# Column norms, split state-space output and set-up, a w_pg begun by quarters, and a later RWKV bonus in a two-block fp32 transformer kernel

## The reference

```python
h = h + rms_norm_2(mix, post_mix_norm[i])
u = rms_norm_2(h, pre_ffn_norm[i])
up = causal_dwconv(u @ w_up[i], conv_w[i], conv_b[i])
f = (gelu(gate) * val) @ w_down[i]
h = h + rms_norm_2(f, post_ffn_norm[i])
e = p[i] @ w_ple[i]
h = h + rms_norm_2(sigmoid(h @ w_ple_gate[i]) * e, ple_norm[i])
```

## Time and profile before

| | us |
|---|---|
| median of the runs | 3297.18 |
| the profiled execution | 3302.57 |
| its span | 3300.5 |
| TensorE busy | 3008.8 (91%) |
| VectorE busy | 2265.7 (69%) |
| ScalarE busy | 1621.3 (49%) |
| GpSimd busy | 324.4 (10%) |

### The profile page before, as it was taken

How to read it: one execution, slowest core, us unless ns; L and a number is a source line. 1 busy time by engine, 2 the same in 40 slices (tenths; PEclk the granted TensorE clock), 3 DMA queues, 4 the chain that set the end, 5 groups by cost and what they waited for, 6 DMA issues and landing times.

```text
span 3300.5 us, 60057 instructions
## 1 busy us (share of the span) xinstructions
PE 3008.8 (91%) x24264; PEld 2777.6 (84%) x24264; DVE 2265.7 (69%) x3538; ACT 1621.3 (49%) x2407; POOL 324.4 (10%) x569
## 2 busy tenths in 40 slices
PE   6799898879998988999898999989899999999987
PEld 2577777768888888999787889989899999999987
DVE  6367776587688876775565566666688855887565
ACT  3345555345466653745343432544555544555554
POOL 0012222100122221300000000010000000000000
PEclk8799999989999998999899998999899999999989
DMA  9876656755644445555232232535355555554543
GB/s 379 287 243 225 203 209 223 253 198 208 162 155 137 139 147 167 176 179 183 89 112 92 100 108 90 173 130 198 128 171 190 179 192 180 179 187 170 180 147 122
DMA packets 110708, 576.94 MB, mean 175 GB/s; under 512 B 33056, under 2 KB 33088, under 8 KB 46688
## 3 DMA queue, kind: packets, MB, share of 16 engines
q1 hardware_dynamic: 89040, 525.37, 45.2%
q0 software_dynamic: 20816, 44.27, 4.7%
q10 hardware_dynamic: 576, 3.47, 0.3%
HBM read 546.83 MB, written 17.83 MB: 171 GB/s over the span
## 4 chain that ended last, share of the span: by engine, by line
PE 60%; DVE 24%; ACT 6%; DMA 5%; issue 3%; SPq 1%; POOL 1%; DVEq 0%; ACTq 0%; POOLq 0%
PE acc L911 59%; DVE arena L871 7%; DVE rounded L871 6%; DVE arena L881 3%; ACT arena L908 2%; DVE upper L871 2%; DMA arena<-in_w_ada 2%; ACT rounded L908 2%; DMA arena<-in_w_in 1%; DVE upper L881 1%; ACT upper L908 1%; PE acc L914 1%; SPq L867 1%; DVE rounded L881 1%; DVE arena L877 1%
## 5 line engine op out<-in xcount | busy, mean ns | idle before, releaser
L911 PE MATMUL acc<-rounded 128*128 128x256 f32 x14688 | 1937.1, 291 | 52.6 <-issue 30.4
L911 PEld LDWEIGHTS acc<-rounded 128*128 128x128 f32 x14688 | 1843.6, 196 | 136.1 <-issue 100.3
L871 DVE TENSOR_TENSOR rounded<-arena,rounded 128x1024 fp32r<-128x1024 f32 (+1 forms) x832 | 1005.3, 1208 | 338.8 <-ACT rounded L908 271.0
L908 ACT ACTIVATE rounded<-arena 128x1024 fp32r<-128x1024 f32 (+1 forms) x864 | 883.6, 1023 | 648.7 <-PE acc L911 489.1
L911 PEld LDWEIGHTS acc<-upper_rounded,rounded 128*128 128x128 f32 x4560 | 565.3, 197 | 45.0 <-DVE rounded L871 22.8
L911 PE MATMUL acc<-upper_rounded,rounded 128*128 128x256 f32 x4560 | 573.1, 289 | 23.1 <-DVE rounded L871 20.7
L908 ACT ACTIVATE arena<-arena 128x256 f32<-128x256 f32 (+4 forms) x477 | 253.0, 530 | 306.0 <-DVE arena L871 213.9
L911 PE MATMUL acc<-arena 128*32 128x512 f32 (+8 forms) x1878 | 267.1, 467 | 79.9 <-DMA arena<-in_w_ada 42.7
L871 DVE TENSOR_TENSOR arena<-arena 128x256 f32<-128x256 f32 (+6 forms) x519 | 273.2, 526 | 51.7 <-ACT arena L908 30.1
L911 PEld LDWEIGHTS acc<-arena 128*32 128x32 f32 (+4 forms) x1878 | 122.8, 139 | 143.9 <-DMA arena<-in_w_ada 67.2
L871 DVE TENSOR_TENSOR arena<-acc,arena 128x256 f32<-128x256 f32 (+3 forms) x280 | 119.1, 425 | 178.0 <-PE acc L911 160.3
(11 more groups left out here) (90 smaller groups left out, 1165.3 us busy)
## 6 DMA issues: line engine op xcount, KB each, us to landing
arena<-in_w_in SPq DMA_DIRECT2D x164, 1024.0 KB, 5.0
arena<-in_w_ada SPq DMA_DIRECT2D x88, 1024.0 KB, 5.3
arena<-in_w_up SPq DMA_DIRECT2D x88, 1024.0 KB, 4.8
arena<-in_w_down SPq DMA_DIRECT2D x44, 1024.0 KB, 4.7
arena<-in_w_outa SPq DMA_DIRECT2D x16, 1024.0 KB, 7.3
arena<-in_w_glu SPq DMA_DIRECT2D x16, 1024.0 KB, 5.4
arena<-in_w_outm SPq DMA_DIRECT2D x16, 1024.0 KB, 5.0
arena<-in_w_out SPq DMA_DIRECT2D x16, 1024.0 KB, 4.8
```

Source lines behind the costliest of these rows:

```text
L871: return self.put(self.e and self.e.tensor_tensor(o, a, b, op))
L908: return self.put(self.e and self.e.activation(o, a, f, scale=scale, **kw))
L911: return self.put(self.e and self.e.matmul(o, l, r, start=start, stop=stop, skip_group_check=True))
```

## The change

- **Columns.** `rms` now multiplies the two halves of RS2 (as the stationary operand) by one column of ones: sums of the 256 tokens come as 128x2. Root and reciprocal work on 128x2 (NCOL). In `recip`, TensorE lays the two columns over all partitions into PSUM bank 3, and scaling reads them there. This holds for the tags (x, 0), mo, fo and em.
- **Early table.** `warm`, a Sqrt of one column, stands behind the first block of tile 15 of w_outm (both layers), w_out2 and w_down1.
- **Interleaving.** `post` is split into `scale` and `post`; the order is scale 0, post 0, scale 1, halves 0, post 1, scale 2, halves 1, and so on, where it was two of both ahead of the first halves.
- **Squares.** The three additions of squares for the w_up norm go from GpSimd to VectorE, as a background program in w_up's first 32 blocks.
- **Quarters.** w_pg's first 64 blocks take four tiles by four blocks of the contraction in turn; its weights are packed so.
- **S5.** Six more steps before block 0; the output is written, read back and passed through gelu in two halves, the first in a generator of its own as soon as block 7 is done; each `s5_out` is split in two parts, 8 steps a tile. Set-up is in 19 parts (two steps each in layer 1, where it was 8 parts; in layer 0 still 8 steps).
- **Bonus.** The bonus product, its multiplication by v and its spill go from stage 2 to stage 3; the subtraction for the exponentials goes from stage 3 to 2.

```diff
-PAIRS = (("w_in", 48), ("w_in2", 0), ("w_up", 0), ("w_pg", 0))
+PAIRS = (("w_in", 48), ("w_in2", 0), ("w_up", 0))
+QUADS = (("w_pg", 0),)
...
+            quads = (name, u0) in QUADS
+            if quads and blk < 64:
+                n, k = n0 + blk // 4 % 4, 4 * (blk // 16) + blk % 4
...
+            if (name, n, k) in (("w_outm", 15, 0), ("w_out2", 15, 0), ("w_down1", 15, 0)):
+                self.add("warm")
...
     def s5(self, l):
-        for i in range(8):
-            self.add("s5_setup", l, i)
-            yield
-            if l:
-                yield
+        for i, parts in enumerate((1, 2, 1, 4, 3, 2, 1, 5)):
+            for part in range(parts):
+                self.add("s5_setup", l, i, part)
+                if l or part == parts - 1:
+                    yield
+                if l:
+                    yield
...
         while ("u8", l, 0) not in self.marks:
             yield
+        for _ in range(6):
+            yield
...
-        self.add("s5_y", l)
-        for _ in range(20):
-            yield
-        for j in range(9):
-            self.add("s5_out", l, j)
...
+    def s5_back(self, l):
+        for half in range(2):
+            while ("s5", l, 8 * half + 7) not in self.marks:
+                yield
+            self.add("s5_y", l, half)
+            for _ in range(14):
+                yield
+            self.add("s5_yr", l, half)
+            for _ in range(8):
+                yield
+            for j in range(4 * half, 4 * half + 4):
+                self.add("s5_out", l, j, 0)
+                for _ in range(3):
+                    yield
+                self.add("s5_out", l, j, 1)
+                for _ in range(2):
+                    yield
+                self.add("part", ("ys", l), j)
+                for _ in range(3):
+                    yield
...
+    def scaled(self, tag, g):
+        if g == 0:
+            self.add("scale", tag, 0)
+        self.add("post", tag, g)
+        if g < 3:
+            self.add("scale", tag, g + 1)
+
+    def square_sums(self):
+        yield
+        for g in range(1, 4):
+            self.add("sum4", g)
+            yield
...
-        for g in range(5):
-            if g < 4:
-                self.add("post", "fo", g)
-            if g:
-                self.add("xs", g - 1)
+        for g in range(4):
+            self.scaled("fo", g)
+            self.add("xs", g)
...
-        pe.mm(B(3, 0, 256), con("ones"), V(RS2, 256), True, True).then_inc("norm_pe", tag)
+        for th in range(2):
+            x = pe.mm(B(3, th, 1), V(RS2 + 128 * th, 128), con("ones", 1), True, True)
+        x.then_inc("norm_pe", tag)
+
+    def recip(tag):
+        if tag in ("x0", "hf"):
+            return
+        pe.wait_ge("norm_dve", ("col", tag))
+        for th in range(2):
+            x = pe.mm(B(3, 128 * th, 128), V(NCOL + th, (0, 128)), con("ident"), True, True)
+        x.then_inc("norm_pe", ("over", tag))
...
-        if s == 2:
+        if s == 3:
             pe.wait_ge("rw_act", ("ld", i))
             pe.wait_ge("rw_dve", ("rk", i))
-            pe.mm(B(4, 0, 256), con("blk"), V(RT2, 256), True, True).then_inc("rw_pe", ("rk", i))
+            pe.mm(B(4, 0, 256), con("blk"), V(D2, 256), True, True).then_inc("rw_pe", ("rk", i))
...
+    def scale(tag, g):
+        src, stream, sem = {"mo": (MO, "w_out2", "ev_act"), "fo": (FO, "w_down1", "g_act"), "em": (EM, "w_pg", "g_act")}[tag]
+        t = V(src + 1024 * g, 4, 256)
+        dve.wait_ge(sem, ("ev", tl.out_of[stream, 0, 4 * g + 3].o))
+        dve.wait_ge("norm_pe", ("over", tag))
+        dve.tt(t, t, B(3, 0, (0, 4), (1, 256)), MUL)
```

More of the change, by code:

```diff
@@ L461, in stream @@
                 held.append(t)
-            if late is not None and blk == 39:
+            if late is not None and blk == (71 if quads else 39):
                 late()
@@ L715, in run @@
             self.stream("w_outa", l, 8 * l, 0, 16, 8, per=2)
-            self.drain(g5)
+            self.drain(g5, gy)
             self.add("glu_first", l)
@@ L1420, in rms, with warm @@
         act.wait_ge("norm_pe", tag)
-        act.act(V(RS, 256), B(3, 0, 256), ACT.Sqrt, bias=con("eps"), scale=1.0 / 2048).then_inc("norm_act", ("sqrt", tag))
+        if total is None:
+            to, sums = V(RS, 256), B(3, 0, 256)
+        else:
+            to, sums = V(NCOL, 2), B(3, 0, 2)
+        act.act(to, sums, ACT.Sqrt, bias=con("eps"), scale=1.0 / 2048).then_inc("norm_act", ("sqrt", tag))
+    def warm():
+        act.act(V(NCOL + 2, 1), con("eps"), ACT.Sqrt)
     def rms2():
@@ L1482, in part, with s5_setup @@
         act.act(to[0], V(src, 256), ACT.Copy).then_inc("part_act", key)
-    def s5_setup(l, i):
+    def s5_setup(l, i, part):
+        if part:
+            return
         if i == 0:
@@ L1857, in h @@
         for j in ([k] if k % 4 == 0 and l == 0 or k == 0 else []) + ([k + 1] if k < last else []):
-            dve.stt(V(UT + 256 * j, 256), V(X + 256 * j, 256), V(GP + j, 1), V(RS, 256), MUL, MUL).then_inc("h_dve", (l, j))
+            if l:
+                dve.wait_ge("norm_pe", ("over", ("x", 0)))
+            root = B(3, 0, 256) if l else V(RS, 256)
+            dve.stt(V(UT + 256 * j, 256), V(X + 256 * j, 256), V(GP + j, 1), root, MUL, MUL).then_inc("h_dve", (l, j))
         dve.wait_ge("h_act", (l, k))
@@ L1878, in part, with s5_setup @@
         low(to, V(src, 256), key)
-    def s5_setup(l, i):
-        if i == 1:
+    def s5_setup(l, i, part):
+        if i == 1 and part == 0:
             dve.wait_ge("s5_act", ("step", l))
@@ L1885, in s5_setup @@
             reduce_angle(V(IM, 64), V(TH, 64), V(T1, 64), 0.0)
+        if i == 1 and part == 1:
             dve.tt(V(TM, 64, 9), V(IM, (1, 64), (0, 9)), V(CON + CCOL["kk9"], (0, 64), (1, 9)), MUL)
             dve.tt(V(PK, 64, 9), V(RE, (1, 64), (0, 9)), V(CON + CCOL["kk9"], (0, 64), (1, 9)), MUL).then_inc("s5_dve", ("arg", l))
-        if i == 3:
+        if i == 3 and part == 0:
             dve.wait_ge("s5_act", ("pk", l))
@@ L1894, in s5_setup @@
             dve.stt(V(EM1, 64), V(EM1, 64), 2.0, V(T1, 64), MUL, MUL)
-            sin_arg(V(P1, 576), V(TM, 576), V(CC1, 576), con("ph1"), con("ph1r")).then_inc("s5_dve", ("p", l, 0))
-        if i == 4:
-            sin_arg(V(P2, 576), V(TM, 576), V(CC1, 576), con("ph2"), con("ph2r")).then_inc("s5_dve", ("p", l, 1))
-        if i == 5:
+        if i == 3 and part == 1:
+            turns_of(V(CC1, 576), V(TM, 576), con("ph1"))
+        if i == 3 and part == 2:
+            turned(V(P1, 576), V(TM, 576), V(CC1, 576))
+        if i == 3 and part == 3:
+            bounded(V(P1, 576), con("ph1r")).then_inc("s5_dve", ("p", l, 0))
+        if i == 4 and part == 0:
+            turns_of(V(CC1, 576), V(TM, 576), con("ph2"))
+        if i == 4 and part == 1:
+            turned(V(P2, 576), V(TM, 576), V(CC1, 576))
+        if i == 4 and part == 2:
+            bounded(V(P2, 576), con("ph2r")).then_inc("s5_dve", ("p", l, 1))
+        if i == 5 and part == 0:
             sin_arg(V(CO, 64), V(IM, 64), V(T1, 64), 0.25, con("hpi")).then_inc("s5_dve", ("trig", l, 0))
+        if i == 5 and part == 1:
             sin_arg(V(SI, 64), V(IM, 64), V(T1, 64), 0.0, con("zero")).then_inc("s5_dve", ("trig", l, 1))
@@ L1905, in s5_setup @@
             dve.tt(V(P2, 576), V(P2, 576), V(PK, 576), MUL)
-        if i == 7:
+        if i == 7 and part == 0:
             dve.wait_ge("s5_act", ("trig", l, 2))
@@ L1915, in s5_setup @@
             dve.recip(V(T1, 64), V(T1, 64))
+        if i == 7 and part == 1:
             dve.tt(V(QR, 64), V(CO, 64), V(ARE, 64), MUL)
@@ L1923, in s5_setup @@
             dve.tt(V(QI, 64), V(QI, 64), V(T1, 64), MUL)
+        if i == 7 and part in (2, 3):
             p1, p2 = V(P1, (9, 64), (1, 8)), V(P2, (9, 64), (1, 8))
             qr, qi = V(QR, (1, 64), (0, 8)), V(QI, (1, 64), (0, 8))
-            for j, (one, two, op) in enumerate(((p1, p2, ADD), (p2, p1, SUB))):
-                dve.tt(V(PQ + 512 * j, 64, 8), one, qr, MUL)
-                dve.tt(V(TM, 64, 8), two, qi, MUL)
-                dve.tt(V(PQ + 512 * j, 512), V(PQ + 512 * j, 512), V(TM, 512), op)
+            one, two, op = ((p1, p2, ADD), (p2, p1, SUB))[part - 2]
+            at = PQ + 512 * (part - 2)
+            dve.tt(V(at, 64, 8), one, qr, MUL)
+            dve.tt(V(TM, 64, 8), two, qi, MUL)
+            dve.tt(V(at, 512), V(at, 512), V(TM, 512), op)
+        if i == 7 and part == 4:
             dve.memset(V(KS, 960, np_=16), 0.0)
@@ L2604, in arrange @@
     order = np.concatenate([n, np.stack([16 + n, 24 + n, 32 + n, 40 + n], 1).reshape(-1), 8 + n])
-    A["w_in"] = np.concatenate([pack(w.reshape(2048, 48, 128)[:, order].reshape(2048, 6144)) for w in g["w_in"]])
+    A["w_in"] = np.concatenate([pack(w.reshape(2048, 48, 128)[:, order].reshape(2048, 6144))
+                                for w in g["w_in"]])
     A["w_outm"] = np.concatenate([pack(w[:1024]) for w in g["w_out"]])
```

160 lines of the change are left out of this document (82 added, 78 removed).

## The result

The changed kernel takes 3261.11 us (median of 4 runs, 3257.28 to 3263.28) against 3296.15 for the kernel before beside it: ratio 0.9889 (95% interval 0.9872 to 0.9906), 1.1% faster. The forecast was 3228, the range 3203 to 3262: the time lies 0.9 us inside the range's upper end, and the gain is half of the forecast one (35 of 69). The profiled execution took 3257.28, its span is 3255.5 against 3300.5: 45.0 us, where 70.5 were forecast.

The account below looks back on a forecast made before the run. TensorE's stream of weight products was bound by holes, most caused by VectorE, plus low clock after them. Terms 15 + 18 + 10 - 6.5 + 11 + 0 + 7.5 + 4.5 + 1 + 10 = 70.5 us off 3297.2; forecast 3228, range 3203 to 3262.

Parts of the forecast that it names:

- rival (a): VectorE is the true bound from 300 to 810 and 885 to 1303 us: 3252 us, chance 0.20.
- what was to show it wrong: Attention stretches longer by over 10 us each, or new waits for w_in in layer 0's first 100 products.
- What the first half costs: First-half gelu puts 12.5 us of VectorE into each attention stretch; 5 us lost in layer 1, 1.5 in layer 0.
- Six more steps: Before the first state-space block: 24 products ahead remove both waits for scr_u; 15 us gained (8 to 19).
- rival (c): State-space chain, shifted against the attention heads, meets their waits in another phase; up to 3315 us, chance 0.03.
- Output in halves: State-space output in w_outa: waits for scr_y and VectorE go; 18 us gained in layer 1, 10 in layer 0.
- Set-up: State-space set-up spread over 19 parts, 678.5 to 810.4 us: VectorE no longer solid; 11 us gained (3 to 19).
- Norm of layer 1's input: Root and reciprocal as columns, against table loads colliding with early sines: 0 (1.6 gained to 3 lost).
- Norms before w_up and w_pg: Earlier scaling and quicker first low halves: 7.5 us gained before w_up (3 to 9), 4.5 before w_pg (2 to 7).
- Tail: Last norm: reciprocal 1.75 becomes 0.18 us, a lay-over is added; 1.0 us gained (0.3 to 1.5).
- Later bonus: RWKV: bonus product one step later shortens TensorE's wait by 1.44 us, exponentials start sooner; 10 us gained (4 to 14).
- (b): Rival: with TensorE's holes the low clock goes too, fifteen us more gained; 3212 us, chance 0.13.

Follow-up runs that it names:

- e5: The kernel before with only the six more steps ahead of the first state-space block: 3297.27 us, ratio 1.0009.
- e6: The changed kernel with the first half's gelu tiles held until the attention's last head is done: 3240.54 us, ratio 0.9827.
- e8: The changed kernel with the first VectorE multiplication of each first-half gelu tile done five times: 3268.62 us, ratio 0.9907.
- e1: The changed kernel without the six steps ahead of the first state-space block: 3260.33 us, ratio 0.9887.
- e7: e6 with the six steps in layer 0 only: 3246.04 us, ratio 0.9841.
- e9: The changed kernel with layer 1's state-space set-up again in 8 parts and 16 steps: 3267.71 us, ratio 0.9904.
- e10: The kernel before with RWKV's subtraction for the exponentials ahead of VectorE's wait for the bonus product, which stays in stage 2: 3285.19 us, ratio 0.9967.

## Why the prediction was right or wrong

The time fell inside the range, but only just, and the mechanism failed in one step. Taken all at their ends, the bounds of the terms give 3192 to 3291, not 3205 to 3250, and the upper end of 3262 came from leaning toward rival (a). Of what was to show it wrong, attention stretches over 10 us longer each, came: 12.5 and 27.5. The other rows gained 85 for the 77 forecast, which hid 8 of the loss.

**What the first half costs** is the step that failed. It said that 12.5 us of VectorE enter each attention stretch and that 5 and 1.5 of them are lost. On their 96 products the four tiles of layer 1 cost 16.0 (e5 and e6 against the changed kernel), those of layer 0 between 11.1 (e6) and 14.9 (e5). I had divided the idle of the whole 352 us stretch, 37 us, where in layer 1 the tiles fall on 55 us in which the kernel before had left VectorE 4 us of air. Even the bound I gave, 12.5, was too low for layer 1. The idle also takes the clock from 0.97 to 0.86, 5.8 of the 16.0, and VectorE stands another 3.23 us for ScalarE in the second tile, a wait that the prediction didn't have. That the loss is made by the tiles where they stand is shown by moving them to where there is room (e6: 0.9827 against 0.9889, and 3240 forecast before it ran). That VectorE's length counts there one for one is shown by adding 7.5 us at the same place (e8: 6.7 and 7.2 lost). What the 3.23 us wait costs by itself was not tried.

**Six more steps** was right for what it named: both waits went, 17.7 with the clock against 15 forecast. As a term of the sum it was wrong, for it ended at those waits. Layer 1's attention stretch gave 10 to 12 back, which was rival (c); in the kernel before, the six steps alone left the time as it was (ratio 1.0009), and in the changed kernel so does their removal (e1). Only with the gelu moved do they seem to pay in layer 1 (5.5 in the medians, e7 against e6, with overlapping intervals). Why four steps cost layer 0 another 20 us stays open; the trace has more waits for ScalarE there (18.6 us against 13.2) at a clock of 0.93, and no rule that I tried foretold it.

**Output in halves**: 34.3 forecast as 28. The debt of VectorE in w_outa of layer 1 was carried by the three halves ahead as worked out; w_glu took 1.6.

**Set-up**: 11.2 forecast as 11, and 12.3 when undone. VectorE is no longer solid in w_glu (51.2 of 62.7).

**Norm of layer 1's input**: the collision of tables came as described, and at the bound named: 3.55 lost of "1.6 gained to 3 lost", 4.65 against what columns alone make (e9: 1.1 gained). The way was another. I had taken the loads to delay the root; it was the squares of the last tiles, queued behind the Sine load and three sines, that came late. The rule of the Trainium skill ("ScalarE: Activation LUTs", What ACT_TABLE_LOAD costs) that was weighed there gave a loss of about 3, near what was measured, but the trace doesn't bear it out as the cause: behind the first two of the three loads the next activation starts within 0.02 us, without a drain beside the 1.28.

**Norms before w_up and w_pg**: 5.3 for 7.5 and 1.7 for 4.5 (3.2 to 3.6 in the profiles of other kernels with this part). The sums of squares left GpSimd and the low halves are short, as forecast:

```profile
2332.76 1.22 DVE L908 TENSOR_TENSOR arena<-arena,acc 128x1024 f32<-128x1024 f32 x1 [1.37 <-PE acc L948]
...
2336.68 2.27 DVE L918 SCALAR_TENSOR_TENSOR rounded<-arena,rounded 128x256 fp32r<-128x256 f32 x4
```

The 1.37 between reciprocal and scaling is the lay-over, which I had sized at 0.5. Before w_pg its four matmuls took 1.07 us (1.23 at layer 1's input), and the first product started 9.8 after w_down instead of 12.1.

```profile
3132.81 1.07 PE L948 MATMUL acc<-arena,upper 128*128 128x128 f32 x4 [0.99 <-DVE upper L926]
...
3139.20 10.89 PE L948 MATMUL acc<-rounded 128*128 128x256 f32 x74 [5.33 <-issue]
```

**Tail**: 0.5 for 1.0.

**Later bonus**: 15.3 in the pair of profiles of the table, 9.2 to 15.3 over all the kernels that have it, for 10. The 1.44 is there to the hundredth in the wait shown, but more than half of the gain in these waits is given back in others, and the exponentials, which I had counted only as the cover for that, make the larger part (e10: 10.8). Right in sum by luck, the larger cause in the smaller clause.

The rivals: (a), VectorE as the true bound, named the mechanism for the attention stretches and gave 12 and 6 where 16 and 11 to 15 came; for the set-up and w_outa of layer 0 it was wrong. (c) holds in layer 1, with 12 of the 31.5 us that it put there. (b) did not come: in the windows above the clock rose where the idle went and fell where idle came, and no gain beyond that shows.

## What to carry to other kernels

A piece of background work costs little only if its engine has room in the very products it falls on: read the window of those products before you divide a stage's idle, and look which of that room is one long wait behind the place, which can't be used (layer 0 here). Look also at what the other engines have queued ahead of each hand-over that the work needs. If TensorE has to wait for it, add the clock to the bill: in layer 1, 5.8 us on top of 10.2 of idle. And a removed wait is a gain only at the end of the chain it started: ask where the same work, started later or earlier, ends.

## What the runs showed of the hardware

- VectorE's busy share hides its gaps. In the changed kernel's window of 71.1 us, 57.35 us of busy time (0.81) in 104 instructions left 8.0 us in waits of over 0.15 us; the other 5.7 us were gaps of 0.03 to 0.14 us between instructions.
- The granted clock fell from 0.97 to 0.86 in a stretch of 71 us in which TensorE's idle rose from 7% to 20%, and the same matmuls (423 and 424 recorded) took 5.8 us longer.
- An early table load (1.28 us) is lost when something of another function stands between it and its use. Here a Sine load and three sines did, and what they delayed was not the root, which found its table, but two squares queued behind them: the gap was 11.12 us with them, 6.06 and 6.47 in the two kernels without.
- The same Sine load and three sines (3.16 us with their gaps) in front of one 0.42 us copy on ScalarE held VectorE for 3.23 us in each attention stretch.
